# The gather of an expert's rows with the token rows stationary and the one-hot moving

## The chip, the cores and the metric

The kernel runs on one core of one Trainium2 chip. The metric is the device time of one execution in microseconds (us). A median is given over several runs; the profile is one execution recorded by the hardware profiler, with a time of its own.

## What is computed

One decoder layer for 256 prompt tokens and 8 sample tokens with width 1024, all in float32: an input projection, a pooling group and an mLSTM group, an output projection and a layer norm, then a mixture of experts, a second layer norm and a gated embedding. Nearly all the time goes into the experts. Each token picks 4 of 32 experts:

```python
logits = xf @ w_router + b_router
top_v, top_e = lax.top_k(logits, TOP_K)          # 4 of 32
gates = jax.nn.softmax(top_v, axis=-1)
# for each expert e and its block of tokens:
h = xb @ w1[e] + b1[e]                           # 1024 -> 2048
glu = jnp.minimum(h[:, ::2], SWIGLU_LIMIT)
lin = jnp.clip(h[:, 1::2], -SWIGLU_LIMIT, SWIGLU_LIMIT)
a = glu * jax.nn.sigmoid(SWIGLU_ALPHA * glu) * (lin + 1)
out = a @ w2[e] + b2[e]                          # 1024 -> 1024
# out * gate is added to the token's row
```

## The kernel before

The kernel is written in Bass: one instruction stream for each engine, ordered by hand, with semaphores between them. The 264 tokens lie in `xtok` as three chunks of 128, 128 and 8 rows, a token to a partition, 1024 elements in each. A block holds up to 64 tokens (`BLOCK`) of one expert.

The weights of an expert are 12 units of 1 MB (`UNITS`): eight for the first product, four for the second. SyncE's queue loads them in order into a ring of 16 slots (L373), each as soon as `units_used` tells that TensorE is done with the slot. So the loads run up to 16 units ahead of TensorE.

TensorE's work for expert n is the function `expert`, called for four experts in each turn of the loop. In order:

- the bias of the first product (L788), then its eight units (L800), each with four matmuls of 512 columns into two PSUM banks. Two half blocks lie side by side in a bank: the partitions 0 to 63 take one half of the columns of the result, 64 to 127 the other, so the stationary operand has 64 columns and two matmuls run side by side in the array. After units 0, 2 and 4 stand the `combine` steps of the expert before (L762, L768), which spread its output over the tokens
- `gather(n + 1)` (L746): the rows of the next expert. The one-hot (a token to a partition, 64 slots) is stationary, the token rows are moving, 512 columns at a time; over three chunks and two halves that makes six matmuls into bank 2, which then holds the gathered rows, a slot to a partition
- `turn_hot` (L753, L754): transposes of the one-hot, for `combine`
- the wait for `act_ready` and four transposes of the activation (L821) into bank 3; ScalarE copies these to `aT` (L1569)
- the wait for `xg_copied` and `turn_gathered` (L775): four transposes of the gathered rows, 128 by 128, into bank 6. They read `xg`, a part of `hist_mix`, to which ScalarE copies bank 2 (L1567)
- the wait for `aT_done`, the bias (L829) and the second product (L839)

VectorE computes the one-hot of the next expert (L1261 to L1266), adds up what `combine` left (L1279, L1284), does the activation (L1303 to L1311) and copies bank 6 to `xgT` (L1272), which is the stationary operand of the next expert's first product; TensorE waits for this copy (`xgT_done`) at the head of `expert`. Ahead of the loop the same steps are done once for expert 0: `gather(0)`, `turn_hot`, `turn_gathered`.

A matmul of float32 shows in the trace as two records, each with a weight load (PEld) of its own; a transpose shows as one.

## Time and profile before

| | |
|---|---|
| median of 3 runs | 1175.5 us (1174.99 to 1177.38) |
| the profiled execution, its own time | 1176.69 us |
| its span, first to last instruction | 1174.7 us |
| TensorE busy (matmul) | 1130.7 us, 96% |
| weight loads | 447.1 us, 38% |
| VectorE, ScalarE, GpSimd busy | 374.6, 162.3, 69.2 us |
| mean granted clock of TensorE | 0.984 |
| HBM | 439.87 MB moved by DMA, 374 GB/s over the span |

How to read it: the busy time of TensorE is that of its matmul records, which are pipelined and overlap, so it says that matmuls follow each other, not that the array works at its peak. The costs of steps are therefore read from the starts of records in the timeline: from the start of one group to the start of the next. The loop over the 32 experts takes the time from some 182 us to 1121 us; ahead of it are the projections, the mixer and the router, behind it the last layer norm and the embedding.

### The profile page before, as it was taken

The page shows a single profiled execution, that of the slowest core. Times are in us where ns is not written, and L with a number is a line of the kernel's source. Part 1 is how long each engine was busy: PE and PEld are TensorE (multiplying, and loading weights), DVE is VectorE, ACT ScalarE, POOL GpSimd, SP SyncE. Part 2 cuts the span into 40 slices and gives each one's busy share as a digit, 9 for nine tenths or more (in the row PEclk, how much of TensorE's full clock was granted, in tenths as well). Part 3 has the DMA queues.
Part 4 walks back from the last instruction along what each step waited for, and adds up shares of the span by engine and source line. Part 5 has one row for each costly group of instructions (what it writes and reads, how often), then busy time and mean ns, then how long its engine had stood idle before and what let it go on. Part 6 is the DMA issues. An engine that isn't in the chain of part 4 may idle for free.

```text
span 1174.7 us, 15244 instructions
## 1 busy us (share of the span) xinstructions
PE 1130.7 (96%) x5771; PEld 447.1 (38%) x5771; DVE 374.6 (32%) x771; ACT 162.3 (14%) x296; POOL 69.2 (6%) x81
## 2 busy tenths in 40 slices
PE   8989979999999999999999999999999999999998
PEld 6878453333333333333333333333333333333334
DVE  1656872222222222222222222222222222222254
ACT  1422121000100010001000101110010000100042
POOL 0734520000000000000000000000000000000000
PEclk9989968999999999999999999999999999999999
DMA  9962796999999999999999999999999999999941
GB/s 316 303 278 84 256 368 243 395 417 418 417 418 418 418 418 418 418 418 417 418 417 418 418 418 417 418 417 418 418 417 418 417 418 418 417 418 417 415 171 38
DMA packets 88464, 439.87 MB, mean 374 GB/s; under 512 B 10446, under 2 KB 11722, under 8 KB 55313
## 3 DMA queue, kind: packets, MB, share of 16 engines
q1 hardware_dynamic: 86969, 435.36, 92.1%
q0 software_dynamic: 1184, 3.71, 1.0%
q10 hardware_dynamic: 288, 0.50, 0.1%
q8 instruction: 13, 0.21, 0.1%
q14 instruction: 10, 0.08, 0.0%
HBM read 436.01 MB, written 3.77 MB: 374 GB/s over the span
## 4 chain that ended last, share of the span: by engine, by line
PE 72%; SPq 19%; DMA 3%; DVE 2%; ACT 2%; issue 2%; DVEq 0%; ACTq 0%
PE bank L800 28%; SPq L373 18%; PE bank L839 14%; PE bank L485 6%; PE bank L746 6%; PE bank L762 4%; DMA ring<-in_w_mlp 2%; PE bank L651 2%; PE bank L921 2%; PE bank L821 1%; ACT wpool L1569 1%; PE bank L788 1%; PE bank L829 1%; PE bank L753 1%; PE bank L768 1%
## 5 line engine op out<-in xcount | busy, mean ns | idle before, releaser
L800 PE MATMUL bank<-ring,proj 128*64 128x512 f32 x2048 | 471.1, 599 | 6.7 <-DMA ring<-in_w_mlp 6.6
L800 PEld LDWEIGHTS bank<-ring,proj 128*64 128x64 f32 x2048 | 135.1, 136 | 295.5 <-issue 247.3
L1279 DVE SCALAR_TENSOR_TENSOR xT<-bank,proj,xT 128x512 f32<-128x512 f32 x128 | 90.2, 747 | 426.0 <-PE bank L762 426.0
L839 PE MATMUL bank<-ring,wpool 128*64 128x512 f32 x1024 | 225.3, 592 | 0.0
L839 PEld LDWEIGHTS bank<-ring,wpool 128*64 128x64 f32 x1024 | 74.0, 137 | 129.1 <-issue 127.3
L746 PE MATMUL bank<-xreg,proj 128*64 128x512 f32 (+1 forms) x396 | 98.1, 613 | 3.6 <-DVE sel L1266 3.6
L1564 ACT ACTIVATE proj<-proj 128x512 f32<-128x512 f32 x32 | 20.2, 631 | 557.1 <-DVE proj L1303 557.1
L485 PE MATMUL bank<-xT,ring 128*128 128x264 f32 x320 | 79.8, 410 | 0.3 <-ACT xT L1425 0.3
L1303 DVE TENSOR_SCALAR proj<-bank 128x256 f32<-128x256 f32 x64 | 24.2, 420 | 162.5 <-PE bank L800 162.5
L762 PE MATMUL bank<-mixT 64*128 64x512 f32 x264 | 74.5, 641 | 0.9 <-ACT mixT L1575 0.9
L485 PEld LDWEIGHTS bank<-xT,ring 128*128 128x128 f32 x320 | 64.6, 204 | 13.6 <-issue 1.7
L746 PEld LDWEIGHTS bank<-xreg,proj 128*64 128x64 f32 (+1 forms) x396 | 25.6, 137 | 69.1 <-issue 65.3
L1575 ACT COPY mixT<-bank 128x512 f32<-128x512 f32 x32 | 18.8, 586 | 229.4 <-PE bank L839 229.4
L762 PEld LDWEIGHTS bank<-mixT 64*128 64x128 f32 x264 | 19.9, 184 | 54.1 <-issue 54.1
L1272 DVE COPY proj<-bank 128x512 f32<-128x512 f32 x33 | 22.8, 692 | 51.2 <-PE bank L775 51.2
L1284 DVE TENSOR_TENSOR hist_mix<-bank,hist_mix 128x128 f32<-128x128 f32 x66 | 16.1, 286 | 53.1 <-PE bank L768 53.1
L651 PE MATMUL bank<-ring,mixT 128*128 128x512 f32 x64 | 28.4, 597 | 0.1
L921 PE MATMUL bank<-ring,mixT 128*128 128x512 f32 (+1 forms) x80 | 28.2, 509 | 0.2 <-DVEq L1352 0.2
L1567 ACT COPY hist_mix<-bank 128x512 f32<-128x512 f32 x32 | 18.8, 587 | 41.6 <-PE bank L746 41.6
L1305 DVE TENSOR_SCALAR proj<-bank 128x256 f32<-128x256 f32 x64 | 23.9, 415 | 0.0
L829 PE MATMUL bank<-bias_parts,sel 96*64 96x512 bf16 x64 | 13.0, 401 | 10.1 <-ACT wpool L1569 10.1
L1308 DVE SCALAR_TENSOR_TENSOR proj<-proj 128x512 f32<-128x512 f32 x32 | 22.2, 694 | 1.1
(309 smaller groups left out, 667.9 us busy)
## 6 DMA issues: line engine op xcount, KB each, us to landing
ring<-in_w_mlp SPq DMA_DIRECT2D x384, 1024.0 KB, 20.1
ring<-in_w_in SPq DMA_DIRECT2D x10, 1024.0 KB, 11.5
ring<-in_w_out SPq DMA_DIRECT2D x4, 1024.0 KB, 9.1
ring<-in_w_ple_gate SPq DMA_DIRECT2D x4, 1024.0 KB, 16.5
xreg<-in_x_prompt SPq DMA_DIRECT2D x4, 512.0 KB, 4.5
ring<-q_row SPq DMA_DIRECT2D x1, 2048.0 KB, 6.7
ring<-k_row SPq DMA_DIRECT2D x1, 2048.0 KB, 6.9
out<-ring POOLq DMA_DIRECT2D x1, 2048.0 KB, 10.9
```

Of the source, the lines that this page charges most:

```text
L373: sp.dma_start(unit_place(s, u), unit_weights(e, u)).then_inc(sem(f"slot{s}"), 16)
L485: last = pe.matmul(bank[t % 2][:, 0:TOK], w[:, k % 4, j * P:(j + 1) * P], xT[:, k, :], start=(k == 0), stop=(k == KD - 1))
L651: last = pe.matmul(banks[half][0:n, :], mixT[:, k, t0:t0 + n], w[:, k % 2, half * 512:half * 512 + 512], start=(k == 0), stop=(k == KD - 1))
L746: last = pe.matmul(bank[2][BLOCK * h:BLOCK * (h + 1), :], onehot[0:m, c, 0:BLOCK], xtok[0:m, c, 512 * h:512 * h + 512], start=(c == 0), st ...
L762: last = pe.matmul(banks[h][:, :], hotT[half, buffer, c * P:(c + 1) * P], eout[half, :], start=True, stop=True)
L800: last = pe.matmul(bank[q][BLOCK * t:BLOCK * (t + 1), :], xgT[:, k % 4, k // 4, :], ring[:, s, col:col + 512], start=False, stop=(k == KD ...
L829: pe.matmul(bank[4][BLOCK * h:BLOCK * (h + 1), :], sel[:, j % 2, :], bias_parts[:, 2 * FF + 512 * h:2 * FF + 512 * h + 512], start=True, s ...
L839: last = pe.matmul(bank[4][BLOCK * h:BLOCK * (h + 1), :], aT[:, m, BLOCK * t:BLOCK * (t + 1)], w[:, k % 2, 512 * h:512 * h + 512], start=F ...
L921: last = pe.matmul(GATE_BANKS[c][i], x2T[:, k, t0:t0 + n], gate_weights(k)[:, PIECES[c][i]], start=(k == 0), stop=(k == KD - 1))
L1279: ins = STT(total[:, c, s], ins_bank[h][:, :], gate_table[:, c, bass.ds(n, 1)], total[:, c, s], ALU.mult, ALU.add)
L1303: TS(glu[:, q, :], hb[q][:, 0, :], LIMIT, None, ALU.min).then_inc(sem("glu_ready"), 1)
L1305: TS(lin[:, q, :], hb[q][:, 1, :], LIMIT, -LIMIT, ALU.min, ALU.max).then_inc(sem("lin_ready"), 1)
```

## The change

`gather` swaps the operands. The token rows are stationary, 128 elements of the width at a time, and the one-hot is moving with its 64 slots. Each matmul gives 128 elements of the width by 64 slots, which is the turned form that `xgT` has. That makes 8 pieces of the width by 3 chunks, 24 matmuls, into bank 6. ScalarE's copies of bank 2, the semaphores `xg_copied` and `xgT_ps`, and `turn_gathered` go; VectorE's copy to `xgT` waits for `gathered` instead.

```diff
             def gather(n):
 
-                for c, (_, m) in enumerate(CHUNKS):
-                    for h in range(2):
-                        last = pe.matmul(bank[2][BLOCK * h:BLOCK * (h + 1), :], onehot[0:m, c, 0:BLOCK],
-                                         xtok[0:m, c, 512 * h:512 * h + 512], start=(c == 0), stop=(c == 2))
+                for k in range(KD):
+                    col = ((k % 4) * 2 + k // 4) * BLOCK
+                    for c, (_, m) in enumerate(CHUNKS):
+                        last = pe.matmul(bank[6][:, col:col + BLOCK], xtok[0:m, c, k * P:(k + 1) * P],
+                                         onehot[0:m, c, 0:BLOCK], start=(c == 0), stop=(c == 2))
                 last.then_inc(sem("gathered"), 1)
...
-            def turn_gathered():
-
-                for q in range(4):
-                    last = pe.transpose(bank[6][:, q * P:(q + 1) * P], xg[:, q, :], ident)
-                last.then_inc(sem("xgT_ps"), 1)
-
...
                 last.then_inc(sem("aT_ps"), 1)
-                pe.wait_ge(sem("xg_copied"), n + 2)
-                turn_gathered()
                 pe.wait_ge(sem("aT_done"), n + 1)
...
             gather(0)
             turn_hot()
-            pe.wait_ge(sem("xg_copied"), 1)
-            turn_gathered()
...
-            pe.wait_ge(sem("xg_copied"), npass * EXPERTS + 1)
             combine(1, (STEP - 1) % 2, LAST_BANKS[1])
...
             def turned(n):
 
-                dve.wait_ge(sem("xgT_ps"), n + 1)
+                dve.wait_ge(sem("gathered"), n + 1)
                 dve.tensor_copy(xgT, bank[6][:, :].rearrange("p (q h s) -> p q h s", q=4, h=2)).then_inc(sem("xgT_done"), 1)
...
-                act.wait_ge(sem("gathered"), n + 2)
-                act.copy(hist_mix[:, 0:512], bank[2][:, :]).then_inc(sem("xg_copied"), 1)
                 act.wait_ge(sem("aT_ps"), n + 1)
```

## Rows read from the trace of the kernel before

**Rows 1.** The page's part 2: 40 equal slices, each digit tenths of full.
```profile
PEclk9989968999999999999999999999999999999999
DMA  9962796999999999999999999999999999999941
```

**Rows 2.** TensorE's timeline, one expert: start us, us busy, line, records [idle before].
```profile
513.83 5.37 PE L800 MATMUL bank<-ring,proj 128*64 128x512 f32 x24
519.03 2.89 PE L746 MATMUL bank<-xreg,proj 128*64 128x512 f32 x12
521.85 0.44 PE L753 MATMUL bank<-cst,proj 128*128 128x128 f32 x2
...
522.37 0.66 PE L821 MATMUL bank<-cst,proj 128*128 128x128 f32 x4
522.87 0.60 PE L775 MATMUL bank<-cst,hist_mix 128*128 128x128 f32 x4
523.78 0.41 PE L829 MATMUL bank<-bias_parts,sel 96*64 96x512 bf16 x2 [0.31 <-ACT wpool L1569]
...
530.88 0.60 PE L788 MATMUL bank<-bias_parts,sel 96*64 96x512 bf16 x4
```

**Rows 3.** The timeline of ScalarE and VectorE in the same expert.
```profile
521.42 0.69 DVE L1311 TENSOR_TENSOR proj<-proj 128x512 f32<-128x512 f32 x1
...
523.07 0.59 ACT L1569 COPY wpool<-bank 128x512 f32<-128x512 f32 x1 [0.52 <-PE bank L821]
523.50 0.69 DVE L1272 COPY proj<-bank 128x512 f32<-128x512 f32 x1 [1.39 <-PE bank L775]
```

**Rows 4.** L829 in four of 32 experts, then TensorE's waits: us, times, longest.
```profile
205.26 0.41 PE L829 MATMUL bank<-bias_parts,sel 96*64 96x512 bf16 x2 [0.31 <-ACT wpool L1569]
...
842.30 0.41 PE L829 MATMUL bank<-bias_parts,sel 96*64 96x512 bf16 x2 [0.31 <-ACT wpool L1569]
...
901.87 0.41 PE L829 MATMUL bank<-bias_parts,sel 96*64 96x512 bf16 x2 [0.31 <-ACT wpool L1569]
...
1113.36 0.41 PE L829 MATMUL bank<-bias_parts,sel 96*64 96x512 bf16 x2 [0.32 <-ACT wpool L1569]
...
PE bank L800 <- DMA ring<-in_w_mlp: 6.6, 16, 1.1
```

**Rows 5.** Weight loads of full-clock stretches ahead of the experts: stationary rows*columns, then moving.
```profile
100.31 0.97 PEld L511 LDWEIGHTS bank<-cst,xreg 128*128 128x128 f32 x8
...
102.99 0.19 PEld L485 LDWEIGHTS bank<-xT,ring 128*128 128x128 f32 x1
...
153.26 1.86 PEld L675 LDWEIGHTS bank<-wrout,xT 128*128 128x128 f32 x16
155.16 0.57 PEld L667 LDWEIGHTS bank<-cst,xreg 8*128 8x128 f32 x8
```

**Rows 6.** The page's part 5: matmuls of 512 columns, stationary 128 by 128.
```profile
L651 PE MATMUL bank<-ring,mixT 128*128 128x512 f32 x64 | 28.4, 597 | 0.1
```

**Rows 7.** TensorE in stretches: us, busy (records), granted clock, DMA share, GB/s.
```profile
39.30:41.70 2.40, 2.38 (x14) 1.00 1.07 369
41.70:45.10 3.40, 3.40 (x8) 0.50 1.12 249
72.40:79.20 6.80, 5.28 (x13) 0.50 0.14 41
...
106.90:112.30 5.40, 5.40 (x49) 1.00 0.02 5
162.20:170.00 7.80, 7.72 (x35) 0.50 1.03 423
```

**Rows 8.** The timeline of the first gather and what follows it.
```profile
173.49 5.58 PE L746 MATMUL bank<-xreg,proj 128*64 128x512 f32 x12 [3.58 <-DVE sel L1266]
179.01 0.69 PE L753 MATMUL bank<-cst,proj 128*128 128x128 f32 x2
...
181.79 1.07 PE L788 MATMUL bank<-bias_parts,sel 96*64 96x512 bf16 x4 [0.85 <-DVE proj L1272]
```

More of the change, by code:

```diff
@@ L245, in build @@
         aT = wpool[:, :, :]
-        xg = hist_mix[:, 0:512].rearrange("p (q d) -> p q d", q=4)
         sample_sum = hist_mix[:, 512:768]
@@ L1579, in _ @@
                 act.activation(total[:, c, :], xtok[:, c, :], ACT.Copy, scale=ALPHA).then_inc(sem("total_ready"), 1)
-            act.wait_ge(sem("gathered"), 1)
-            act.copy(hist_mix[:, 0:512], bank[2][:, :]).then_inc(sem("xg_copied"), 1)
             act.nop().then_inc(sem("out_done"), 1)
```

## The prediction

> **What bounds the kernel now.** I first read the page's slices [rows 1]. From the seventh on the DMA digit is 9, and the clock digit is 9 nearly throughout. So in the loop over the experts two things look full at once, the loads and TensorE, and the page can't say which one sets the pace. The timeline can. The bias matmul L829 comes once in an expert, and its start is a good mark [rows 4]. From 205.26 to 842.30 us lie 22 experts, so one takes 28.956 us. From 901.87 to 1113.36 lie seven, 30.2 us each. TensorE's waits say what changed: it waited for loads 16 times, 6.6 us in all, about two for each of the last eight experts, those that take longer. So for two thirds of the loop TensorE sets the pace alone. The loads can only keep up one expert in 30.2 us; in these 22 experts TensorE eats up the lead of the ring, and then the loads bind. This gives the rule for every cost below: an expert that becomes faster than 28.96 us only reaches the load bound sooner and ends at about the same time, while one slower than 30.2 us is paid in full 32 times.
>
> Next I read one expert [rows 2, 3]. Gather starts at 519.03, `turn_hot` at 521.85, the activation's transposes at 522.37, `turn_gathered` at 522.87, L829 at 523.78, the next expert at 530.88. There is no idle time ahead of any of them but L829, which waited 0.31 us for ScalarE's copy of `aT`. So what is added to the gather moves everything behind it.
>
> **What the change removes.** The old gather goes: 2.82 us from start to start (519.03 to 521.85) [rows 2]. `turn_gathered` goes too, and looks like half a microsecond. But L829 doesn't wait for it. It waits for the copy L1569, which starts at 523.07 and ends at 523.66 [rows 3], and this copy waits for L821. The time from L821 to L829 is 522.37 to 523.78, 1.41 us, and it holds the four transposes as filling. Without them the same 1.41 us stand, with some 0.8 us idle instead of 0.31. I take nothing for them in the loop. ScalarE's copy L1567 of the gathered rows (one an expert) is beside TensorE's work and frees nothing that anyone waits for: ScalarE was idle 0.52 us ahead of the `aT` copy [rows 3]. VectorE's copy L1272 at 523.50 has until the next first product at 530.88 [rows 2, 3]. It now waits for `gathered`, with `comb_read` of the next expert queued behind it on VectorE; the gather ends before L821, so the copy can only come sooner. The activation's end at 522.11 (L1311) lay 0.26 us ahead of L821 [rows 2, 3], and with a longer gather it is covered all the more. Bank 6 was last read by that same copy an expert earlier, and TensorE waits for that at the head of `expert`; no wait is added there. These edits cost and give nothing.
>
> **What it adds.** 24 matmuls, 48 records, each with a stationary operand of 128 columns and a moving one of 64 columns. No such form is in the trace, so I look for the nearest. Between 100.31 and 102.99 us stand 24 weight loads in a row at the full clock (eight each of L511, L517 and L520), with 1, 128 and 1 moving columns by turns [rows 5]. That is 2.68 us / 24 = 0.1117 us for a record, and it is the same for 1 and for 128 columns: the weight load sets it, and the moving columns are hidden under it. The router's (L675) 16 with 32 moving columns go from 153.26 to 155.16, 0.119 us each [rows 5]. 64 lies between 1 and 128, so I take 0.1117 us: 48 x 0.1117 = 5.36 us for the gather, 2.54 us more than before. The Trainium skill has a rule for this ("TensorE: Matmul & The Clock Gate", section "LDWEIGHTS (loading the stationary operand)"): a load costs its columns divided by 1.2 in ns, whatever the number of rows. By that rule, as an estimate, 48 x 106.7 ns = 5.12 us, and the total would be 1242 instead of 1250.
>
> The bounds. Sixteen of the 48 records have only 8 rows. Eight loads of 8 rows by 128 columns (L667, transposes) took 0.57 us, with 0.14 us for the last one some 0.062 us apart [rows 5]. If the sixteen went at this pace, the gather would save 16 x 0.050 = 0.8 us of the 2.54. Upper bound: the router's 0.119 us gives 48 x 0.007 = 0.35 us more. I stay with 0.1117 for all, since the row of L667 is of transposes, which have one record where a matmul has two.
>
> **The loop.** The new expert takes 28.956 + 2.54 = 31.50 us. That is over 30.2 us, so the loads no longer bind anywhere, and what they cost before comes back: first to last L829 took 908.10 us, 31 experts at 28.956 are 897.6, so 10.5 us return. The 32 gathers in the loop add 32 x 2.54 = 81.3 us.
>
> **Ahead of the loop.** The first gather ran at the half clock, 173.49 to 179.01, 5.52 us [rows 8]. The new one at half clock is 48 x 0.223 = 10.7 us, 5.2 us more. Here `turn_gathered` was on the path: from the end of the gather to L788 passed 2.78 us (179.01 to 181.79) [rows 8]. Without it VectorE's copy (0.69 us) [rows 3] can start with the gather's end, some 0.9 us with the handovers, so 1.9 us return. In all +3.3 us. Behind the loop nothing changes: TensorE waits for no load there.
>
> **Sum.** 1174.7 - 10.5 + 81.3 + 3.3 = 1248.8 us of span. The profiled execution was 2.0 us longer than its span (1176.69), so 1250.8; the median of the runs shown is 1.2 us below it, so **1250 us**, in round numbers, 6.3% slower. With the bounds of the record's cost: 0.8 us less an expert gives 1224, 0.35 us more gives 1261.
>
> **Rival A: the clock falls in every expert.** The clock was granted in full in the loop [rows 1]. The new gather puts 5.4 us of small matmuls, a third of them on 8 rows, next to the transposes and 0.8 us idle. In the trace the clock went to half at 41.70 although TensorE was busy all the time: the 2.4 us before it were 13 records on 4 rows [rows 7]. It also stayed at half from 162.2 to 170.0 while TensorE was busy with small matmuls of 32 columns [rows 7]. Against it: from 106.90 to 112.30 the clock stayed full [rows 7], and that stretch was weight-load bound, with 128 and 1 moving columns by turns, which is as many columns in a microsecond as 64 throughout. But all its records had 128 rows. After a fall the clock was at half for 3.4 us (41.70 to 45.10) or 6.8 us (72.40 to 79.20) [rows 7]. If it is half as fast for that long, an expert loses 1.7 to 3.4 us: 1250 + 32 x 1.7 = 1304 up to 1250 + 32 x 3.4 = 1359, middle 1332. The Trainium skill ("TensorE: Matmul & The Clock Gate", section "A second HAM failure mode: psum-queue depth-cycling") tells of a kernel whose clock swung between its two levels though its idle times were short. In the loop of before no row shows such a swing.
>
> **Rival B: only the streamed columns count, and nothing changes.** If the weight loads hide wholly, as they do for wide matmuls, a record costs its columns. 512 columns on 128 by 128 took 28.4 / 64 = 0.444 us a record [rows 6], so 64 cost 0.055 us, and 48 of them 2.66 us, 0.16 us less than the old gather. The loads would then bind a little sooner, and the end stays where it is: 1173 to 1177 us. The point from which this decides is a gather of some 4.0 us (2.82 + 30.2 - 28.96), 0.084 us a record: below it the loads swallow the added time nearly whole, above it each 0.1 us costs 3.2 us. Against it speak all the rows 5, none of which with 128 stationary columns in a float32 matmul is below 0.11 us. The same page's section "Back-to-back issue gap" gives some 25 ns as the floor for such small matmuls; as an estimate that is 1.2 us for the gather, and the total would be that of this rival.
>
> **How the numbers follow.** The forecast (1250 us, own range 1224 to 1262) gets 0.60. Rival A (1304 to 1359) gets 0.32: its nearest rows point both ways. Rival B gets 0.05, of which 0.01 is faster by over 0.2%. 0.03 is left for something that I don't see, on the slow side. The range must reach into A to hold 8 in 10: 1226 to 1345 leaves out a little below, the upper third of A, and B. A change of under 0.2% could hardly be told from none here. Faster 0.01, same 0.04, slower 0.95.
>
> **What would show it.** The gather's group (now forms 128*128 and 8*128 with 64 columns, 48 records an expert) should take 5.4 us from its start to `turn_hot`; L829 should come every 31.5 us from first to last expert, without the step to 30.2; its idle time should grow from 0.31 to some 0.8 us; TensorE's waits for loads should be gone, and the DMA digits fall below full now and then. In rival A the clock slices show less than 9 in the loop and the second product (7.1 us) is stretched. In rival B the starts of L829 stay at 28.8 and then 30.2. The forecast is wrong if records on 8 rows are cheap or if the 64 columns are not hidden.

## The result, and the profile after

The change makes the kernel slower, by far more than I forecast: the median is 1476.24 us (four runs, 1468.1 to 1478.91) against 1175.32 us before. The ratio is 1.254, with a 95% interval of 1.249 to 1.260. The prediction was 1250 us with a range up to 1345. The ratios in this document leave out executions that took over 1.5% longer than the fastest of the same kernel; that matters only for the kernel without the transposes, below.

The page of the changed kernel, parts 1, 2 and 5; the second line of slices is the granted clock:

```profile
span 1477.1 us, 17315 instructions
...
PE 1428.5 (97%) x6827; PEld 705.3 (48%) x6827; DVE 375.1 (25%) x771; ACT 142.9 (10%) x263; POOL 69.2 (5%) x81
...
PE   8999899999999999999999999999999999999998
...
PEclk9999578888888888888888888888888888888889
DMA  9846768888787887887878878878888888788500
...
L746 PE MATMUL bank<-proj,xreg 128*128 128x64 f32 (+1 forms) x1584 | 313.7, 337 | 3.6 <-DVE sel L1255 3.6
```

TensorE is busy 97% of a much longer span. The clock digit, 9 throughout the loop before [rows 1], is 8 in nearly all slices of it, and the loads, full before, have gaps. The gather alone has 313.7 us of busy time. Its timeline for one expert (start, us busy, line, records, [idle time before]):

```profile
629.75 9.17 PE L746 MATMUL bank<-proj,xreg 128*128 128x64 f32 x48
638.85 0.69 PE L753 MATMUL bank<-cst,proj 128*128 128x128 f32 x2
639.46 0.27 PE L754 MATMUL bank<-cst,proj 8*128 8x8 f32 x1
639.67 1.11 PE L815 MATMUL bank<-cst,proj 128*128 128x128 f32 x4
641.53 0.64 PE L821 MATMUL bank<-bias_parts,sel 96*64 96x512 bf16 x2 [0.75 <-ACT wpool L1556]
641.95 8.82 PE L831 MATMUL bank<-ring,wpool 128*64 128x512 f32 x32
650.60 0.60 PE L782 MATMUL bank<-bias_parts,sel 96*64 96x512 bf16 x4
```

Against [rows 2]: the gather takes 9.10 us (629.75 to 638.85) instead of 2.82; from there to the bias matmul (L821 now, L829 before) 2.68 instead of 1.93; and the second product, which the change doesn't touch, 9.07 (641.53 to 650.60) instead of 7.10. So three stretches grew, by 6.28, 0.75 and 1.97 us. The next lines are the first and the last L821, then three stretches of the expert above (us, TensorE busy, records that ran in the stretch, granted clock, DMA share, GB/s):

```profile
218.09 0.64 PE L821 MATMUL bank<-bias_parts,sel 96*64 96x512 bf16 x2 [0.75 <-ACT wpool L1556]
...
1411.16 0.64 PE L821 MATMUL bank<-bias_parts,sel 96*64 96x512 bf16 x2 [0.75 <-ACT wpool L1556]
```

```profile
630.00:635.30 5.30, 5.30 (x36) 1.00 1.03 410
635.30:645.50 10.20, 9.45 (x33) 0.50 0.42 169
645.60:667.80 22.20, 22.20 (x116) 1.00 0.94 388
```

An expert takes (1411.16 - 218.09) / 31 = 38.49 us, where 29.29 was the mean before [rows 4]. The clock falls to half 5.5 us into the gather, while TensorE is busy without a gap, and stays there for 10.2 us, over the rest of the gather, the transposes and the first ten of the 32 records of the second product. This happens in all 32 experts; the stretches at half last 10.2 us in 23 of them and 13.7 us in nine. The whole difference: the first bias matmul is 12.8 us later than before, the 31 experts behind it take 285.0 us more (1193.07 against 908.10), and the end 4.6 us more, 302.4 us in all.

So rival A happened, but far beyond its price, and something else is wrong too. At the full clock, too, the gather was slower than 0.1117 us a record would have it: 34 records started in the first stretch of 5.3 us (its x36 counts two more that were still running), where 47 would have. Two questions follow: what makes the records dearer, and what makes the clock fall. In the notes below a piece is the gather's work for 128 elements of the width: two matmuls on 128 rows and one on 8 rows, six records. The starts of the six within the full-clock part of the trace are 0.16, 0.11, 0.11, 0.21, 0.16 and 0.20 us apart, 0.95 us a piece instead of 0.67.

### The profile page after: what moved, and what is told of

Same layout as the page of the kernel before. It is cut to its first block, busy times and chain, and to the rows that moved or that the text cites. A ratio compares the mean times of both kernels' runs of the same rounds, so it can differ in the third digit from the quotient of the medians.

```text
span 1477.1 us, 17315 instructions
## 1 busy us (share of the span) xinstructions
PE 1428.5 (97%) x6827; PEld 705.3 (48%) x6827; DVE 375.1 (25%) x771; ACT 142.9 (10%) x263; POOL 69.2 (5%) x81
## 4 chain that ended last, share of the span: by engine, by line
PE 94%; DVE 2%; ACT 2%; DMA 1%; issue 1%; SPq 0%; DVEq 0%; ACTq 0%
PE bank L794 31%; PE bank L746 21%; PE bank L831 19%; PE bank L762 5%; PE bank L484 5%; PE bank L815 2%; PE bank L650 1%; PE bank L910 1%; PE bank L753 1%; PE bank L821 1%; ACT wpool L1556 1%; PE bank L782 1%; PE bank L768 1%; DVE xreg L1057 1%; PE bank L876 0%
## 5 line engine op out<-in xcount | busy, mean ns | idle before, releaser
L746 PE MATMUL bank<-proj,xreg 128*128 128x64 f32 (+1 forms) x1584 | 313.7, 337 | 3.6 <-DVE sel L1255 3.6
L746 PEld LDWEIGHTS bank<-proj,xreg 128*128 128x128 f32 (+1 forms) x1584 | 266.3, 229 | 70.8 <-issue 26.0
L831 PE MATMUL bank<-ring,wpool 128*64 128x512 f32 x1024 | 289.5, 729 | 0.0
L831 PEld LDWEIGHTS bank<-ring,wpool 128*64 128x64 f32 x1024 | 90.1, 171 | 183.3 <-issue 182.3
L1556 ACT COPY wpool<-bank 128x512 f32<-128x512 f32 x32 | 18.8, 586 | 312.0 <-PE bank L815 312.0
L821 PE MATMUL bank<-bias_parts,sel 96*64 96x512 bf16 x64 | 20.3, 631 | 24.0 <-ACT wpool L1556 24.0
L815 PE MATMUL bank<-cst,proj 128*128 128x128 f32 x128 | 35.7, 434 | 0.0
```

Source lines behind the costliest of these rows:

```text
L746: last = pe.matmul(bank[6][:, col:col + BLOCK], xtok[0:m, c, k * P:(k + 1) * P], onehot[0:m, c, 0:BLOCK], start=(c == 0), stop=(c == 2))
L815: last = pe.transpose(bank[3][:, m * P:(m + 1) * P], act_out[:, m * P:(m + 1) * P], ident)
L821: pe.matmul(bank[4][BLOCK * h:BLOCK * (h + 1), :], sel[:, j % 2, :], bias_parts[:, 2 * FF + 512 * h:2 * FF + 512 * h + 512], start=True, s ...
L831: last = pe.matmul(bank[4][BLOCK * h:BLOCK * (h + 1), :], aT[:, m, BLOCK * t:BLOCK * (t + 1)], w[:, k % 2, 512 * h:512 * h + 512], start=F ...
L1556: act.copy(aT, bank[3][:, :].rearrange("p (m s) -> p m s", m=4)).then_inc(sem("aT_done"), 1)
```

## The experiments

Each kernel is the changed one unless said otherwise, with the edit shown. The kernel before took 1166.5 to 1181 us on the same chips. Times without a ratio are of one execution each, the profiled one. How often the clock falls can differ between executions of one kernel, as the kernel without the transposes will show, so small differences in the number of falls prove little.

**The third chunk on 128 rows.** The 8 rows of the samples become 128; the one-hot is zero in the others.

```diff
-                    for c, (_, m) in enumerate(CHUNKS):
-                        last = pe.matmul(bank[6][:, col:col + BLOCK], xtok[0:m, c, k * P:(k + 1) * P],
-                                         onehot[0:m, c, 0:BLOCK], start=(c == 0), stop=(c == 2))
+                    for c in range(3):
+                        last = pe.matmul(bank[6][:, col:col + BLOCK], xtok[0:P, c, k * P:(k + 1) * P],
+                                         onehot[0:P, c, 0:BLOCK], start=(c == 0), stop=(c == 2))
```

> The changed kernel, but the third chunk's matmuls run on all 128 partitions instead of 8; the rows beyond the 8 samples meet a one-hot of zeros. The work and the number of records are the same, 48 in a gather; only their rows change. In the changed kernel's trace a piece of the gather (128, 128 and 8 rows, two records each) has its starts 0.16, 0.11, 0.11, 0.21, 0.16 and 0.20 us apart, 0.95 us in all at the full clock, and some 5 us in, the clock falls to half for 10.2 or 13.7 us. Theory S+R (each change between 128 and 8 rows costs time by itself, and the clock falls because a third of the records feed 8 rows and the rest only 64 columns under a load of 0.11 us): all records 0.112 us apart, 5.4 us a gather, the clock stays full as in the stretch of before that was bound by weight loads on 128 rows, an expert 31.5 us, time near 1250 us. Theory L (any stretch of 5 us that is bound by weight loads makes the clock fall): records 0.112 us apart at first, but the clock falls in every expert, an expert 34 to 36 us, 1330 to 1400 us. Theory W (rows don't matter, a record with 64 moving columns costs 0.16 us): 1470 us as the changed kernel.

Measured 1253.48 us (before: 1168.16). The timeline and a stretch inside the gather:

```profile
330.00 5.57 PE L746 MATMUL bank<-proj,xreg 128*128 128x64 f32 x48
335.41 0.39 PE L753 MATMUL bank<-cst,proj 128*128 128x128 f32 x2
...
337.29 0.41 PE L821 MATMUL bank<-bias_parts,sel 96*64 96x512 bf16 x2 [0.75 <-ACT wpool L1556]
337.52 7.04 PE L831 MATMUL bank<-ring,wpool 128*64 128x512 f32 x32
344.39 0.60 PE L782 MATMUL bank<-bias_parts,sel 96*64 96x512 bf16 x4
```

```profile
330.10:335.10 5.00, 5.00 (x46) 5.00 (x46) 1.00 1.02 410
```

The gather takes 5.41 us, 0.113 a record (45 starts in the 5 us), and the clock is full in the whole loop. An expert takes 31.59 us. The same 48 records with more rows fed are 223 us faster than in the changed kernel. That is theory S+R within 4 us, and it drops L (this is a stretch of over 5 us in which the weight loads never pause, at the full clock) and W. S and R are taken away together here; the next kernels part them.

**Without the third chunk.**

```diff
-                    for c, (_, m) in enumerate(CHUNKS):
+                    for c, (_, m) in enumerate(CHUNKS[0:2]):
...
-                                         onehot[0:m, c, 0:BLOCK], start=(c == 0), stop=(c == 2))
+                                         onehot[0:m, c, 0:BLOCK], start=(c == 0), stop=(c == 1))
```

> The changed kernel without the third chunk in the gather: 16 matmuls, 32 records, all on 128 rows. The rows of the 8 sample tokens are left out, so the experts see zeros for them. Theory S+R (the price lies in the changes between 128 and 8 rows, and the clock falls for the weak records): 32 x 0.112 = 3.6 us a gather, an expert 29.7 us by TensorE, so the loads bind at 30.2 and the time is 1176 to 1182 us, the clock full in the loop. Theory L (a stretch bound by weight loads makes the clock fall): 3.6 us of it and the transposes and the idle time behind it, the clock falls in some or all experts, an expert 31 to 34 us, 1230 to 1330 us.

Measured 1191.48 us (before: 1168.16). The gather takes 3.62 us and the clock is full, as S+R said, but the time is 10 us over what I expected. An expert takes 29.81 us from the first to the last, and TensorE waits for no load in the loop. I had taken the loads' pace of 30.2 us for a floor under the loop; it isn't (see the kernel with one more pair).

**Twice the moving columns.**

```diff
-                    col = ((k % 4) * 2 + k // 4) * BLOCK
+                    col = (k % 4) * P
...
-                        last = pe.matmul(bank[6][:, col:col + BLOCK], xtok[0:m, c, k * P:(k + 1) * P],
-                                         onehot[0:m, c, 0:BLOCK], start=(c == 0), stop=(c == 2))
+                        last = pe.matmul(bank[(6, 2)[k // 4]][:, col:col + P], xtok[0:m, c, k * P:(k + 1) * P],
+                                         onehot[0:m, c, :], start=(c == 0), stop=(c == 2))
```

> The changed kernel with 128 moving columns instead of 64 in each matmul of the gather (the one-hot's other 64 columns repeat the first), into two banks, and VectorE's copy in two halves, each from one bank. The same 48 records and the same changes of rows, twice the streamed columns. Theory R (the clock falls because too little streams through the array; the load of 128 columns hides 64 moving columns and hides 128 just as well): the gather's starts stay as they are at the full clock, 0.95 us a piece, 7.6 us in all, the clock stays full or falls less, an expert 33.7 us, time 1320 to 1330 us, faster than the changed kernel although more is computed. Theory S' (the fall comes from the many changes between 128 and 8 rows): the clock falls as before, 1476 us or more.

Measured 1361.86 us, against 1478.91 for the profiled execution of the changed kernel: twice the streaming, 117 us less. Stretches of the gather and of a second product, columns as before:

```profile
373.90:382.00 8.10, 8.10 (x47) 1.00 1.02 410
...
419.20:422.60 3.40, 3.40 (x12) 0.51 0.00 0
```

The gather is longer than expected, 8.44 us instead of 7.6 (373.82 to 382.26): the first record behind each change of rows now costs 0.21 instead of 0.16 us, so an expert at the full clock takes 34.68 us, and the time lies over R's 1320 to 1330. But the clock stays full in 23 of 32 experts and falls for 3.4 us in nine. The 15 changes of rows are all still there, so S' is dropped: they alone don't make the clock fall. Of R the direction holds, a gather with more moving columns keeps the clock up in most experts, and its price doesn't.

**Grouped by chunks.** The loops of the gather exchanged, one change of rows instead of 15.

```diff
-                for k in range(KD):
-                    col = ((k % 4) * 2 + k // 4) * BLOCK
-                    for c, (_, m) in enumerate(CHUNKS):
+                for c, (_, m) in enumerate(CHUNKS):
+                    for k in range(KD):
+                        col = ((k % 4) * 2 + k // 4) * BLOCK
                         last = pe.matmul(bank[6][:, col:col + BLOCK], xtok[0:m, c, k * P:(k + 1) * P],
-                                         onehot[0:m, c, 0:BLOCK], start=(c == 0), stop=(c == 2))
+                                         onehot[0:m, c, 0:BLOCK], start=(c == 0 and k == 0),
+                                         stop=(c == 2 and k == KD - 1))
```

> The changed kernel with the two loops of the gather exchanged: all eight matmuls of the first chunk, then eight of the second, then eight of the third on 8 rows. The same 48 records, but one change of rows instead of 15. Theory S (the changes between 128 and 8 rows cost the time over 0.112 us a record): 48 x 0.112 = 5.4 us a gather at the full clock. Theory E (a record on 8 rows is dearer by itself): 32 x 0.112 + 16 x 0.16 = 6.1 us. For the clock: the 16 weak records now stand together at the end, 1.8 us, next to the transposes and the idle time. If the mean over a few microseconds counts, it falls in every expert all the same and the time is 1330 to 1420 us; if it stays full, 1250 us.

Measured 1362.84 us. Stretches of the gather that starts at 203.63: first the part on 128 rows (here a second pair of columns gives the weight loads' busy time), then up to the fall, then at half.

```profile
203.70:207.20 3.50, 3.50 (x32) 3.50 (x32) 1.00 1.04 425
...
203.60:208.60 5.00, 5.00 (x45) 1.00 1.03 421
208.70:215.50 6.80, 6.05 (x23) 0.50 0.48 190
```

Forty-three records of the gather start in the first 5 us; those on 8 rows follow each other 0.112 us apart like the others. Where the clock holds until the gather's end it takes 5.64 us, 0.23 us over that on 128 rows: 0.14 for the change to 8 rows, and 0.09 for the first part of the change back, ahead of `turn_hot`. So theory S is right and E is wrong, a record on 8 rows costs nothing extra by itself. But the clock falls in every expert, and the kernel with one change in its gather is still 109 us slower than that on 128 rows. So the clock falls without the many changes too. The stretches at half are shorter than in the changed kernel (6.8 us in 21 experts, 10.2 in eight, 3.4 in three).

**64 rows, and 72 rows, in the third chunk.**

```diff
-                    for c, (_, m) in enumerate(CHUNKS):
+                    for c, m in enumerate((P, P, 72)):
```

> The changed kernel with the third chunk's matmuls on 72 partitions instead of 8 or 128; the rows beyond the 8 samples meet a one-hot of zeros. With 8 rows each change of rows cost some 0.14 us (a piece took 0.95 us instead of 0.67) and the clock fell in every expert; with 128 rows neither. Theory T (the cost of a change comes with the small tile of the array that 8 rows use, and 72 rows take the whole array): all records 0.112 us apart, 5.4 us a gather, an expert 31.6 us; the clock stays full, as 72 rows feed the array much more than 8: 1250 to 1257 us. Rival R72 (the cost comes with any change in the number of rows): 0.95 us a piece, an expert 33.8 us or more, over 1320 us. Rival K (no changes cost, but the clock falls in some experts because the third chunk feeds only half of the rows): 1270 to 1360 us.

Measured 1263.8 us with 72 rows.

> As the kernel with 72 rows in the third chunk, but with 64. With 72 the records stood 0.112 us apart throughout (5.41 us a gather) and the clock fell in 6 of 32 experts; with 8 a piece took 0.95 us instead of 0.67. Theory T (the price of a change comes with a smaller tile of the array, and 64 rows are a tile of half the array, as in the combine steps): a piece takes 0.95 us again, 7.6 us a gather, an expert 33.8 us at the full clock; some falls of the clock on top; 1325 to 1390 us. Rival T' (the price comes only with tiles far from the full one, or with the 8 rows as such): 5.4 us a gather, falls in a few more experts than with 72 rows, 1255 to 1290 us.

Measured 1478.61 us with 64 rows. A stretch inside the gather of each, the one with 72 rows first (TensorE busy, weight loads busy, clock):

```profile
867.50:872.00 4.50, 4.50 (x42) 4.50 (x42) 1.00 1.03 411
```

```profile
631.00:635.50 4.50, 4.50 (x30) 3.84 (x29) 1.00 1.03 409
```

In 4.5 us start 40 records with 72 rows and 28 with 64 (the views count two more that were still running). 72 rows go at the pace of 128, and 64 at that of 8, and the 64 rows kernel is the changed kernel over again, time, spacing (0.95 us a piece) and falls (10.2 or 13.7 us in every expert). For the price of a change that is theory T. Of the times, 72 rows took 7 us more than its range and 64 rows 89 us more: the expectations let the clock fall too little. The six falls with 72 rows are rival K's, below its range of 1270 to 1360. With 72 rows the clock fell in six of 32 experts for 3.4 us; its bias matmuls stand (1198.97 - 211.13) / 31 = 31.87 us apart, 0.27 us over those of 128 rows. Here the pace of the records is that of 128 rows and only fewer rows are fed, so the rows alone may have made these falls; with one execution of each kernel, six falls against none don't prove it. The next kernel shows it better.

**Grouped, with 64 rows.**

```diff
-                for c, (_, m) in enumerate(CHUNKS):
+                for c, m in enumerate((P, P, 64)):
                     for k in range(KD):
```

> The kernel grouped by chunks (one change of rows in a gather, 5.64 us at the full clock) with 64 rows instead of 8 in the third chunk's 16 records. The spacing stays the same, only the rows fed change. Grouped with 8 rows: the clock fell in every expert, 34.92 us an expert, 1363 us. Theory Q (the rows fed count for the clock): it falls in fewer experts or for shorter, 31.9 to 33.5 us an expert, 1260 to 1320 us. Theory Z (rows don't count, a small tile counts as weak whatever its rows): as grouped, 1350 to 1370 us.

Measured 1310.1 us. Same pace as grouped (5.64 us where the clock holds), but 53 us less: an expert takes (1245.31 - 205.86) / 31 = 33.53 us instead of (1295.10 - 212.45) / 31 = 34.92, and the clock holds in six experts and falls for only 3.4 us in 16. Theory Q, though an expert is a little above the top of its range, 33.5. The rows fed count; they are one of several things, since 64 rows at a pace of 0.95 us a piece gained nothing.

**The gather spread over the units,** with the third chunk on 8 rows, then on 128. `gather` takes the numbers of the pieces to do, two at a time.

```diff
                     elif k == 4:
                         combine(2, (j + 1) % 2)
+                        pe.wait_ge(sem("onehot_ready"), n * 3 + 6)
+                    if k >= 4:
+                        gather(n + 1, range(2 * (k - 4), 2 * (k - 4) + 2))
 
-                pe.wait_ge(sem("onehot_ready"), n * 3 + 6)
-                gather(n + 1)
```

> The changed kernel with its gather cut up: two pieces (of 128, 128 and 8 rows) behind each of the units 4 to 7 of the first product instead of all eight pieces in a row behind unit 7. The same 48 records with the same changes between 128 and 8 rows, but never more than 2 us of them without wide matmuls between. Theory C (two causes: a change of rows costs time wherever it stands, 7.6 us a gather instead of 5.4; and the clock falls when such weak work stands together for some microseconds): the clock stays full, some 7.6 us are added for the pieces, an expert 33.7 us, time near 1322 us. Theory S' (the changes themselves make the clock fall): 1400 to 1476 us. If the changes were free next to wide matmuls: 1253 us.

Measured 1426.3 us, far over theory C and within the range of S'.

> The same cut-up gather, with the third chunk on all 128 partitions: no change of rows, and no weak records. With all 128 rows and the gather in one piece an expert took 31.59 us and the kernel 1253.5 us at the full clock. Theory C: spreading moves the records and saves nothing more, since the clock was full already: 31.5 to 31.7 us an expert, 1250 to 1257 us. Theory H (weight loads next to wide matmuls hide under them, so a piece costs only its streamed columns, 0.055 us a record): 48 x 0.055 = 2.7 us instead of 5.4, an expert 28.9 us, the loads bind, 1170 to 1177 us.

Measured 1390.68 us, 137 us more than with the gather in one piece, which no theory had. Its timeline and the wait that was not there before (engine, waited for: us in total, times, longest); ahead of them one part of the gather with 8 rows (spread), then with 128, and the unit behind each:

```profile
441.82 1.97 PE L746 MATMUL bank<-proj,xreg 128*128 128x64 f32 x12
443.72 1.94 PE L800 MATMUL bank<-ring,proj 128*64 128x512 f32 x8
```

```profile
628.03 1.55 PE L746 MATMUL bank<-proj,xreg 128*128 128x64 f32 x12
629.51 1.94 PE L800 MATMUL bank<-ring,proj 128*64 128x512 f32 x8
631.38 1.55 PE L746 MATMUL bank<-proj,xreg 128*128 128x64 f32 x12
```

```profile
639.47 0.39 PE L759 MATMUL bank<-cst,proj 128*128 128x128 f32 x2
...
641.12 0.66 PE L822 MATMUL bank<-cst,proj 128*128 128x128 f32 x4 [1.11 <-DVE proj L1307]
642.53 0.42 PE L828 MATMUL bank<-bias_parts,sel 96*64 96x512 bf16 x2 [0.75 <-ACT wpool L1563]
```

```profile
PE bank L822 <- DVE proj L1307: 35.6, 32, 1.1
```

The whole gather behind the last unit was also the cover of VectorE's activation, which lasts from the last unit's end to 522.11 in [rows 2, 3], about 2.9 us. With only two pieces left there, TensorE waits 1.11 us for it, then 0.75 for the copy, with nothing but transposes around. In this stretch or right behind it the clock falls in every expert, for 3.4 us in 16 and 6.8 in 16. The spread gather itself gained nothing: its starts next to wide matmuls are the 0.112 us of the others, so H is wrong. It even lost. Two pieces on 128 rows take 1.48 us (628.03 to 629.51) where 12 x 0.1117 are 1.34, and the unit behind them 1.87 us (629.51 to 631.38) where the pace of [rows 2] gives 8 x 5.20 / 24 = 1.73. So going from the gather's matmuls (stationary 128 by 128) to the units' (128 by 64) costs some 0.14 us, and so does going back, with 128 rows on both sides. Three more parts make six such changes, some 0.9 us an expert or 28 us. With the waits of 35.6 us and 164 us at half, worth up to 82, that makes 146, an estimate from above for the 137.

With 8 rows two pieces take 1.90 us (441.82 to 443.72), 0.95 a piece as in the changed kernel: the changes of rows cost the same next to wide matmuls. That the time fell into the range of S' doesn't bear S' out. The clock held in four of 32 experts with all changes in them, and with no change of rows it fell in all 32.

**The old gather without the transposes.** The kernel before, with only the removed half of the change.

```diff
                 last.then_inc(sem("aT_ps"), 1)
-                pe.wait_ge(sem("xg_copied"), n + 2)
-                turn_gathered()
                 pe.wait_ge(sem("aT_done"), n + 1)
...
-                dve.wait_ge(sem("xgT_ps"), n + 1)
+                dve.wait_ge(sem("gathered"), n + 1)
...
-                act.wait_ge(sem("gathered"), n + 2)
-                act.copy(hist_mix[:, 0:512], bank[2][:, :]).then_inc(sem("xg_copied"), 1)
```

> The kernel before with its old gather, without the four transposes and ScalarE's copy of the gathered rows; VectorE's copy waits for the gather alone. The experts' rows are left out by this: the copy takes what the bank held. It measures what the removed half of the change was worth by itself. Theory P (as predicted): nothing in the loop, since L829 waits for the copy of aT, 1.41 us from L821 to L829 as before, its idle time 0.31 growing to 0.75 to 0.82; ahead of the loop some 1.9 us. An expert 28.96 us. As the loads had no room before the first expert frees its slots, the end comes 0 to 2 us sooner: ratio 0.998 to 1.000. Rival: the transposes cost 0.5 us an expert on TensorE, 28.4 us, and the loads bind earlier: ratio 0.995 to 0.999 and more waits for loads.

Ratio 1.0056 (1.0004 to 1.0108), and ten executions between 1171.37 and 1193.47 us, the profiled one 1192.34: without the transposes it is not faster, and if anything a little slower (the shortest 1171.37 against 1167.10). The mean granted clock was 0.958 to 0.974 in these ten, 0.980 to 0.988 in the thirteen of the kernel before, so it was lower in every one, by amounts that differ. The profiled execution (0.961) is one of the lower ones. Two experts of it, one with and one without a fall, and the clock behind the first:

```profile
415.94 0.66 PE L821 MATMUL bank<-cst,proj 128*128 128x128 f32 x4
417.34 0.41 PE L827 MATMUL bank<-bias_parts,sel 96*64 96x512 bf16 x2 [0.75 <-ACT wpool L1562]
417.58 8.74 PE L837 MATMUL bank<-ring,wpool 128*64 128x512 f32 x32
...
599.57 0.41 PE L827 MATMUL bank<-bias_parts,sel 96*64 96x512 bf16 x2 [0.75 <-ACT wpool L1562]
599.80 7.04 PE L837 MATMUL bank<-ring,wpool 128*64 128x512 f32 x32
```

```profile
412.60:417.80 5.20, 4.45 (x25) 1.00 1.02 406
417.80:421.20 3.40, 3.40 (x10) 0.50 1.03 410
```

Where the clock holds, an expert takes 28.96 us, and from L821 to L827 pass 1.40 us, as predicted. But in 16 of 32 experts the clock falls when the second product has just begun, for 3.4 us, and the product takes 8.8 us instead of 7.1. The four transposes cost no time because they filled a wait, and with them the clock stays up. That it is the filling that does it is the plain reading; the experts also compute on other values here, and that rival was not tested. The Trainium skill ("TensorE: Matmul & The Clock Gate", section "Part 4: PE-mode transpose") says that transposes don't count for the clock as other matmuls do. Here the clock fell in half of the experts once four of them were taken away, so in this kernel they seem to count.

**Grouped, with filling.** Four more transposes behind those of L815.

```diff
                 last.then_inc(sem("aT_ps"), 1)
+                for m in range(4):
+                    pe.transpose(bank[2][:, m * P:(m + 1) * P], act_out[:, m * P:(m + 1) * P], ident)
```

> The kernel grouped by chunks with four more transposes of the activation (into bank 2, which nobody reads) behind the four of L815, where turn_gathered stood before. They fill the time in which TensorE waits for the copy of aT. The kernel before without these transposes let the clock fall in 16 of its 32 experts, for 3.4 us each time. Theory F (the lost filling is what makes the clock fall, in this form of the gather too): the clock falls in few experts, near 1260 us. Theory G (the fall in the grouped kernel comes 4.5 to 6 us after the gather's start, within its 16 records on 8 rows or right behind them and ahead of the place of the filling; so the weak records are the cause there): the clock falls in every expert as in the grouped kernel, 1340 to 1363 us; at most the stretch at half gets shorter in some experts.

Measured 1329.71 us against 1362.84 for grouped: both theories in part, and below the range of G. The clock still falls in 31 experts, but for shorter (14 falls of 3.4 us, the others 6.8, none of 10.2), 164 us at half in all instead of 235. More transposes, 33 us less. So filling gives back a part of the 109 us. It isn't needed where the records have all their rows: the kernel on 128 rows has the same wait, unfilled, and its clock holds.

**One more pair.** The kernel before, with a longer old gather.

```diff
             def gather(n):
 
+                for h in range(2):
+                    pe.matmul(bank[2][BLOCK * h:BLOCK * (h + 1), :], onehot[:, 0, 0:BLOCK],
+                              xtok[:, 0, 512 * h:512 * h + 512], start=True, stop=True)
                 for c, (_, m) in enumerate(CHUNKS):
```

> The kernel before with two more wide matmuls in each gather (the first chunk's pair twice, the second time with a fresh start, so the result is the same): one pair, 0.94 us at the full clock, an expert 29.8 to 29.9 us by TensorE. It measures from which point a longer gather is paid. As I put it in the prediction (an expert is only paid in full above 30.2 us, since the loads bind there): some 1176 us, ratio 1.00 to 1.002. Theory M (the loads' pace binds only after the ring's lead is used up, and the mean of before was 908.1 / 31 = 29.29 us an expert; whatever goes over that mean is paid, as the kernel without the third chunk, with 29.81 us an expert, took 1191 us): 31 x 0.55 = 17 us more, ratio 1.014 to 1.017. If nothing were hidden: 32 x 0.9 = 29 us, 1.025.

Ratio 1.0111 (1.0050 to 1.0172), 1189.1 us. The pair (L745) costs 0.86 us, and the later wait for loads is gone:

```profile
616.73 1.03 PE L745 MATMUL bank<-xreg,proj 128*64 128x512 f32 x4
617.59 2.89 PE L749 MATMUL bank<-xreg,proj 128*64 128x512 f32 x12
620.41 0.44 PE L756 MATMUL bank<-cst,proj 128*128 128x128 f32 x2
```

An expert takes (1129.20 - 204.93) / 31 = 29.82 us. My rule of the prediction is excluded (1.00 to 1.002); theory M's 1.014 to 1.017 lies within the interval, and the shortest executions (1184.91 and 1167.10 us) give 1.015. The profiled execution fits it: 0.53 us an expert over the mean of 29.29 [rows 4] are 16 us, and the profiled ones are 1192.5 and 1176.7.

**The head kept warm.** The kernel before, with six wide matmuls where TensorE waits ahead of the loop.

```diff
+            def warm_array(b, count):
+                for _ in range(count):
+                    pe.matmul(b[:, :], ident, xtok[:, 0, 0:512], start=True, stop=True)
...
                 c = ORDER[i]
+                if i == 2:
+                    warm_array(bank[1], 1)
...
+                if i:
+                    warm_array(bank[1], 1)
                 pe.wait_ge(sem("x1T_done"), 2 * i + 2)
...
+            warm_array(bank[2], 3)
             pe.wait_ge(sem("onehot_ready"), 3)
             gather(0)
```

> The kernel before with six wide matmuls (128 by 128 on 512 columns, their results are overwritten) at places where TensorE waits ahead of the loop: one ahead of the last chunk's transposes in the router, one ahead of each of the waits for x1T of the last two, and three ahead of the wait for the first one-hot. In the kernel before the clock is at half from 157.7 to 185.0 us, TensorE waits 3.6 us ahead of the first gather, and the gather takes 5.5 us instead of 2.8; the loads stand still from about 177 to 186 us since no slot gets free before the first expert. Theory V (the clock stays full or rises before the first gather; the first expert starts 3 to 5 us sooner, the loads resume sooner by as much, and the end with them): ratio 0.995 to 0.998. Rival U (the fillers come in the way of the router, or the clock falls all the same): ratio 1.000 to 1.003.

1162.73 us, ratio 0.9937 (0.9899 to 0.9974): faster than the kernel before by 0.6%, or by 0.4% if the shortest executions are compared (1161.39 and 1166.50 us). The profiled execution:

```profile
172.25 2.94 PE L755 MATMUL bank<-xreg,proj 128*64 128x512 f32 x12
...
177.39 0.63 PE L797 MATMUL bank<-bias_parts,sel 96*64 96x512 bf16 x4 [0.85 <-DVE proj L1282]
```

The first gather takes 2.87 us instead of 5.52 [rows 8] and the first expert starts at 177.39 instead of 181.79. Theory V; the ratio is a little beyond its range, that of the shortest executions, 0.996, in it. The mechanism of the change is not needed for it, only what the experiments showed of the clock: work without a result, in a wait, can pay.

## Why the prediction was wrong, point by point

**What bounds the kernel.** Right for what was forecast: TensorE sets the pace, and in the changed kernel its waits for loads are gone. The rule that I drew from it was wrong: it took 30.2 us an expert, the loads' pace, as the point from which a longer gather is paid. In the kernel before, the loads bind only in the last quarter of the loop, and the whole took 29.29 us an expert. A gather that brings the expert over that mean is paid at once, as the kernels without the third chunk (29.81 us, 1191 us) and with one more pair (29.82 us, ratio 1.011) show. Rival B's point of 4.0 us for a gather was wrong by it; by the mean, as an estimate, it is 2.82 + 29.29 - 28.96 = 3.15 us.

**The price of a record.** The step that failed first. 0.1117 us, read from [rows 5], is right for records on 128 rows: 0.113 measured, and the kernel with 128 rows in all chunks took 1253.5 us, where the sum gave 1250, and 31.59 us an expert, where it gave 31.50. By the rule of the Trainium skill ("TensorE: Matmul & The Clock Gate", section "LDWEIGHTS (loading the stationary operand)") the gather was estimated at 5.12 us; the trace of that kernel has 5.41, nearer to the row's 5.36. For the changed kernel the term was mis-sized, 5.36 instead of 8 x 0.95 = 7.6 us at the full clock. I had looked at whether the sixteen 8-row records were cheaper, and not at the 15 changes between 128 and 8 rows. These cost some 0.14 us each (0.28 us a piece with two changes), with 64 rows as with 8. The price stood in the rows that I had: in [rows 2] 24 records of the units take 5.20 us, so twelve should take 2.60, and the old gather, of the same shape but for its 8-row chunk, takes 2.82. In its trace the pair of records ahead of the change takes 0.53 us and the one behind it 0.48, where the others take 0.43. So 512 moving columns don't hide the change either. The same section of the Trainium skill says that the number of rows doesn't matter to a load; the traces agree for one load (0.112 us on 8 rows as on 128). The price is in the change from one to the other.

**That the clock holds.** The forecast's second failure, and the larger one. Rival A named the mechanism, the rows and the place, and I gave it 0.32. It happened in every expert, and the sum's full clock is the term that failed most. Of the 225 us between the kernel on 128 rows and the changed one (profiled executions), the pace of the gather explains 32 x 2.18 = 70 us at the full clock; the rest is the clock. Rival A's size was off as well: 1304 to 1359 us against 1476. I took the lengths of 3.4 and 6.8 us at half from two falls that were followed by wide matmuls [rows 7]. Here a fall in the middle of the gather about doubles what is left of it, with 0.21 to 0.35 us between starts, and the clock comes back only after 10.2 or 13.7 us. That it comes back later because the weak work lasts longer is argued, not shown. The row that I held against A, 106.90 to 112.30 at the full clock, had 128 rows in all records and no changes, and is the likeness of the kernel with 128 rows, not of the changed one.

**The transposes at nothing.** In time this was right: 1.40 us from L821 to L827 without them, 28.96 us an expert where the clock holds. As for cover it was wrong. I named what hides their cost, and forgot that they themselves were filling: in the profiled execution without them the clock falls in 16 of 32 experts of the kernel before. What this adds to the loss of the changed kernel is not shown; the kernel on 128 rows lacks them too, at the full clock. The idle time of 0.75 us ahead of the bias matmul came as predicted.

**Ahead of the loop.** +3.3 us predicted; the first product starts at 186.97 instead of 181.79, 5.2 us later. The gather at half took 13.28 us (172.77 to 186.05) instead of 10.7. The changes of rows account for it: on 128 rows in all chunks the same gather at half took 10.30 us.

**The sum, by steps that were run.** The weight loads of 48 records on 128 rows: from 1175 to 1253.5 us, the step that was predicted (the profiled span is 1251.7 us, 77.0 over that of before, where the sum gave 74.1). Sixteen of them on 8 rows, grouped, so that the clock falls in all experts: to 1362.8, 109 us more. The changes of rows in every piece, 1.95 us an expert at the full clock (7.59 against 5.64) or 62 us, and with them longer stretches at half: to 1478.9, 116 us more. The other 54 us fit the clock: the stretches at half in the loop add up to 358 us in the changed kernel and 235 us in the grouped one, and 123 us more at half speed are worth up to 61 us, as an estimate.

**What stays open.** What exactly the clock answers to. Rows fed (8, 64, 72, 128), moving columns (64, 128), the pace of the records and filling in the waits each went with a change of it, most of them in a single execution. No run isolates a law of it.

## What to carry to other kernels

Turning a gather by exchanging its operands trades a few wide matmuls for many narrow ones, and then the weight load is the price: count records by the load, not by the moving columns, and keep all chunks on the full array even if rows are zero. Before work is taken out of a wait, ask what it does for the clock: here four transposes that cost no time went with a full clock, and six matmuls without a result saved about 0.5%. And a step that is moved (the spread gather) uncovers what stood beside it, and pays again at each of its new borders.

## What the runs showed of the hardware that I had not expected

- In float32 matmuls with 128 stationary and 64 moving columns, a change between 128 rows and 8 or 64 rows costs about 0.14 us; between 128 and 72 rows nothing (a gather of 5.41 us with either). A change between 128 and 64 stationary columns costs as much (six more of them in the spread gather), and 512 moving columns don't hide the change of rows (the old gather). Records of the same kind follow each other 0.112 us apart on 8 rows as on 128.
- Rows of zeros were cheaper than fewer rows: 128 rows in the third chunk instead of 8, 1253.5 against 1478.9 us.
- The clock fell to half in the midst of uninterrupted TensorE work, 4.4 to 6.1 us into the gather, in all 32 experts, and came back after 10.2 or 13.7 us. With 72 rows in the third chunk it fell in six experts, with 128 in none, in one execution each.
- In the loop of the kernel before the clock fell once four transposes were taken out of a wait: in 16 of 32 experts of the profiled execution.
